# Recurrent heads on one weighted buffer, and modulation units inside the MLP streams

## Chip, cores and metric

The kernel is one launch on one core of a Trainium2 chip. Five engines run side by side: TensorE multiplies matrices from SBUF into PSUM (eight banks), VectorE and ScalarE work on elements, GpSimd does a few element operations, and SyncE issues the DMAs. The metric is the device time of one execution in microseconds (us), lower is better.

## What is computed

Two transformer blocks on 256 tokens of width 2048, all in fp32. The first block has an input projection, a mixing stage (Fourier mixing on half of the width, dilated attention with eight heads on the other), an output projection and an MLP of width 8192. The second has context and latent tokens, a modulation computed from `c`, bidirectional recurrent heads (four GLA heads and four mLSTM heads), and a gated MLP with a 3x3 convolution. Cut to what the change touches:

```python
mod = (c_act @ w_mod + b_mod)                 # 2048 x 12288; the same for c_ctx
sh1, sc1, gt1, sh2, sc2, gt2 = jnp.split(mod, 6, axis=-1)
h = rmsnorm(x, g_norm1) * (1 + sc1) + sh1     # projections q, k, v, gates
# GLA, per direction, head and chunk, a decay per position and channel:
rel = jnp.where(tril, bcum[j] - bcum[i], -inf)
scores[j, i] = sum_k q[j, k] * k[i, k] * exp(rel[j, i, k])
o = scores @ v + (q * exp(bcum)) @ s
s = exp(b_end) * s + (k * exp(b_end - bcum)).T @ v
# mLSTM: the same with one scalar gate per position, a running maximum
# and a normaliser:
s = (q @ k.T) * exp(d_log - m_q)
h = (s @ v + inter * (q @ c)) / max(|den|, exp(-m_q))
y = rmsnorm(o) * g * silu(gate)               # mLSTM: sigmoid(gate)
x = x + gt1 * (y @ w_out)
x = x + gt2 * conv_ffn(rmsnorm(x) * (1 + sc2) + sh2)
```

The modulation does not depend on the first block, so `w_mod` may be read and multiplied at any time before the second block needs it.

## The kernel before

**Streams.** All large products are streams of weight tiles of 128 x 1024 fp32 (512 KB). SyncE asks for each tile in program order into a ring `raw` of eight slots. ScalarE copies it to `whi` (a rounded high part, line 967), VectorE subtracts to `wlo` (line 1289), and TensorE makes three products for each pair (lines 461 to 463: high by high, low by high, high by low). A tile's slot is free again when TensorE has used the tile (`tile_used`), and the ring is one sequence over all streams and fills: the tile at place q waits until the tile at q - 8 is used. A block is 8 tiles. The first MLP consists of four up streams (`up1_0` to `up1_3`) and four down streams (`dn1_0` to `dn1_3`) of 32 tiles each, in blocks of 8.

**Modulation units.** The product with `w_mod` is cut into 48 units. A unit is four unsplit tiles (2 MB): TensorE multiplies them with 16 matmuls of 256 columns into one PSUM bank (`mod_tiles`, line 475), ScalarE copies the row to `modrow` (`mod_rows`, line 975), TensorE turns it into columns (`mod_columns`, line 483), and VectorE adds the bias into `modT` (`mod_adds`, line 1217). Units stand in fills, between streams: 2 at the start, 10 in the mixing stage, 7 ahead of the first MLP, 7 in the context states and 22 in the heads.

**Order.** There is no scheduler: each engine has its program, written by hand, and the engines meet by semaphores. What stands ahead on an engine is done first, also when what stands behind is ready.

**Heads.** `heads2` exists once for each engine. For the GLA heads it goes through 14 levels, seven (`LEVELS`) for each direction z: at level n, blocks of 2L = 2^(n+1) positions are weighted by the decay measured from their middle. VectorE subtracts the middle from the running decay `bT` (line 1512), ScalarE takes the exponential of the negative absolute value (line 1131), VectorE multiplies the queries (`qE`, line 1537) and GpSimd the keys (`kE`, or in `zl`, line 1692), TensorE makes the scores of all four heads and both token tiles (line 801, eight matmuls of 128 x 128), and VectorE takes the masked part of them into `ST` (line 1499). After each level stands one unit. After the seventh level the state that comes from the context is made (lines 827 to 830) and the running decay of the other direction is built (line 779). Then come the GLA output (lines 843 to 845), the q and k transposes and gate rows of the mLSTM heads (lines 708 to 862) and eight mLSTM steps, one for each head and direction. A step broadcasts a head's rows (874), multiplies keys and queries (878), weights them on VectorE (1598, 1605), makes the output (893, 894), scales it on VectorE (1578 to 1588), and has one unit (475) up to the seventh. Then come the gain and gate products (1627) and the transposes for `out2` (582).

## Time and profile before

| | us |
|---|---|
| median of three runs | 2799.53 (2797.16 to 2802.60) |
| the profiled execution | 2801.47 |
| its span on the core | 2799.7 |
| in1, from the first weight product | 29.95 to 213.8 |
| mixing stage | 215.6 to 312.8 |
| ahead of the first MLP | 402.9 to 446.4 |
| first MLP | 446.4 to 1190 |
| heads | 1676.6 to 1927.4 |
| in these, mLSTM steps | 1814.1 to 1903.1 |
| mean granted TensorE clock | 0.965 of full speed |

All numbers are of one profiled execution, apart from the median. In the rows below a timeline row gives the start, the length, the engine, the line of the kernel, the operation with what it writes and reads, and in brackets how long the engine was idle before it and whom it waited for. Several instructions of one kind in succession are one row, with their number behind x. A window row gives the busy time of each engine in a stretch and TensorE's mean granted clock, 1.00 for full speed.

### The profile page before, as it was taken

The numbers are of one execution on the slowest core, as the hardware profiler recorded it, in microseconds if no ns is written. First come the engines' busy times: TensorE is split into PE (matmuls) and PEld (weight loads), VectorE is DVE, ScalarE is ACT, GpSimd is POOL, SyncE is SP. The second block draws the span as 40 slices with busy tenths as digits, with TensorE's granted clock in tenths as the row PEclk, the third lists the DMA queues.
The fourth block names the chain that finished last, engine by engine and source line by source line (L and its number), as shares of the span: only waits on it lengthen the run. The fifth ranks groups of instructions, "written<-read, shape, count | busy, mean of one in ns | idle before, by whom it ended". The sixth has DMA issues, their size and how long they took to land.

```text
span 2799.7 us, 39040 instructions
## 1 busy us (share of the span) xinstructions
PE 2628.4 (94%) x16120; PEld 2254.8 (81%) x16120; DVE 1483.8 (53%) x1836; ACT 1081.7 (39%) x1294; POOL 40.9 (1%) x18
## 2 busy tenths in 40 slices
PE   6999898999999999999799996787989999999997
PEld 4886577989889899778578884556889979998996
DVE  4433435544545545553354436436577766775675
ACT  4433324433434344453344333303433343334333
POOL 0000000000000000000000003200000000000000
PEclk9999998999999999999899998887999999999999
DMA  7552766555555556455545555544535555555554
GB/s 285 192 193 111 295 238 228 183 189 185 187 185 185 188 183 234 151 188 188 214 139 191 192 195 213 190 181 145 186 129 184 183 187 197 183 185 185 184 177 132
DMA packets 143883, 529.17 MB, mean 189 GB/s; under 512 B 16112, under 2 KB 16112, under 8 KB 142464
## 3 DMA queue, kind: packets, MB, share of 16 engines
q1 hardware_dynamic: 143744, 527.17, 54.2%
q8 instruction: 105, 1.72, 0.2%
q14 instruction: 34, 0.28, 0.0%
HBM read 525.01 MB, written 2.10 MB: 188 GB/s over the span
## 4 chain that ended last, share of the span: by engine, by line
PE 88%; DVE 5%; DMA 3%; ACT 2%; issue 1%; SPq 0%; DVEq 0%; ACTq 0%
PE PSA L461 26%; PE PSA L462 26%; PE PSA L463 26%; DMA raw<-in_w_mod 3%; PE PSA L475 2%; PE PSA L801 1%; DVE cv L1267 1%; PE PSA L893 1%; DVE wlo L1289 1%; DVE tpv L1374 1%; PE PSA L582 1%; DMA raw<-in_w_in 1%; ACT whi L967 1%; PE PSA L619 1%; PE PSA L631 0%
## 5 line engine op out<-in xcount | busy, mean ns | idle before, releaser
L1289 DVE TENSOR_TENSOR wlo<-raw,whi 128x1024 fp32r<-128x1024 f32 x788 | 925.5, 1219 | 529.1 <-ACT whi L967 526.4
L967 ACT ACTIVATE whi<-raw 128x1024 fp32r<-128x1024 f32 x788 | 795.2, 1051 | 550.8 <-DMA raw<-in_w_down 209.1
L461 PE MATMUL PSA<-uhi,whi 128*128 128x256 f32 x2400 | 681.8, 284 | 3.2 <-issue 2.8
L462 PE MATMUL PSA<-ulo,whi 128*128 128x256 f32 x2400 | 681.3, 284 | 0.0
L463 PE MATMUL PSA<-uhi,wlo 128*128 128x256 f32 x2400 | 681.3, 284 | 0.0
L461 PEld LDWEIGHTS PSA<-uhi,whi 128*128 128x128 f32 x2400 | 463.0, 193 | 4.6 <-issue 3.4
L462 PEld LDWEIGHTS PSA<-ulo,whi 128*128 128x128 f32 x2400 | 463.0, 193 | 0.2
L463 PEld LDWEIGHTS PSA<-uhi,wlo 128*128 128x128 f32 x2400 | 463.0, 193 | 0.0
L461 PE MATMUL PSA<-whi,uhi 128*128 128x512 f32 x1088 | 432.9, 398 | 27.4 <-DVE wlo L1289 15.5
L462 PE MATMUL PSA<-wlo,uhi 128*128 128x512 f32 x1088 | 430.2, 395 | 0.0
L463 PE MATMUL PSA<-whi,ulo 128*128 128x512 f32 x1088 | 429.7, 395 | 0.0
L461 PE MATMUL PSA<-whi,ahi 128*128 128x512 f32 x856 | 338.4, 395 | 3.6 <-DVE wlo L1289 3.6
L463 PE MATMUL PSA<-whi,alo 128*128 128x512 f32 x856 | 337.8, 395 | 0.0
L462 PE MATMUL PSA<-wlo,ahi 128*128 128x512 f32 x856 | 337.8, 395 | 0.0
L461 PEld LDWEIGHTS PSA<-whi,uhi 128*128 128x128 f32 x1088 | 208.3, 191 | 74.0 <-issue 24.1
L463 PEld LDWEIGHTS PSA<-whi,ulo 128*128 128x128 f32 x1088 | 208.3, 191 | 44.2
L462 PEld LDWEIGHTS PSA<-wlo,uhi 128*128 128x128 f32 x1088 | 208.6, 192 | 43.2
L461 PEld LDWEIGHTS PSA<-whi,ahi 128*128 128x128 f32 x856 | 161.2, 188 | 42.9 <-issue 5.2
L463 PEld LDWEIGHTS PSA<-whi,alo 128*128 128x128 f32 x856 | 161.1, 188 | 37.9
L462 PEld LDWEIGHTS PSA<-wlo,ahi 128*128 128x128 f32 x856 | 161.2, 188 | 37.2
L475 PE MATMUL PSA<-raw,cst 128*32 128x256 f32 x1536 | 113.6, 424 | 46.5 <-DMA raw<-in_w_mod 31.2
L1267 DVE SCALAR_TENSOR_TENSOR cv<-PSA,vec,cv 128x189 f32<-128x189 f32 (+2 forms) x344 | 133.0, 427 | 16.9 <-DVE cv L1258 1.8
(254 smaller groups left out, 1418.8 us busy)
## 6 DMA issues: line engine op xcount, KB each, us to landing
raw<-in_w_up SPq DMA_DIRECT2D x300, 512.0 KB, 3.3
raw<-in_w_in SPq DMA_DIRECT2D x208, 512.0 KB, 3.2
raw<-in_w_mod SPq DMA_DIRECT2D x192, 512.0 KB, 7.1
raw<-in_w_down SPq DMA_DIRECT2D x192, 512.0 KB, 3.2
raw<-in_w_out SPq DMA_DIRECT2D x64, 512.0 KB, 3.2
raw<-in_w_down2b SPq DMA_DIRECT2D x20, 512.0 KB, 3.7
h<-in_x SPq DMA_DIRECT2D x2, 1024.0 KB, 6.2
xc<-in_ctx SPq DMA_DIRECT2D x2, 1024.0 KB, 9.1
```

Source lines behind the costliest of these rows:

```text
L461: pe.matmul(dst, xh, wh, start=start, stop=False)
L462: pe.matmul(dst, xh, wl, start=False, stop=False)
L463: return pe.matmul(dst, xl, wh, start=False, stop=stop)
L475: mm = pe.matmul(PSA[32 * j:32 * j + 32, bank, 0:UW], cst[:, 2 * k:2 * k + 32], raw[:, q % SLOTS, j * UW:(j + 1) * UW], start=t == 0, stop ...
L582: mm = pe.transpose(PSA[:, banks[n % 4], kk * TOK + t * P:kk * TOK + (t + 1) * P], src, ident)
L619: mm = pe.matmul(PSA[:, c, :], z1[:, t, s * 256 + c * P:s * 256 + (c + 1) * P], cB("dft_pos")[:, t * 512:(t + 1) * 512], start=t == 0, sto ...
L801: mm = pe.matmul(PSA[:, b0 + c // 4, (c % 4) * P:(c % 4 + 1) * P], lk(hd, slice(t * P, (t + 1) * P)), lq[:, hd, t * P:(t + 1) * P], start= ...
L893: pe.matmul(dst[:, c], WW[:, r % 2, t, jc * P:(jc + 1) * P], rhs, start=n == 0, stop=False)
L967: AF(whi[:, n % SLOTS, 0:w], raw[:, n % SLOTS, 0:w], ACT.Copy).then_inc(hi_done, 1)
L1267: last = STT(cvv[n][:, ro, co], gate[n][:, ri, ci], cwv[:, ck + n, tap:tap + 1], cvv[n][:, ro, co], ALU.mult, ALU.add)
L1289: TT(wlo[:, n % SLOTS, 0:w], raw[:, n % SLOTS, 0:w], whi[:, n % SLOTS, 0:w], ALU.subtract).then_inc(lo_done, 1)
L1374: ins = TS(buf[:, n % 2, kk * TOK:(kk + 1) * TOK], PSA[:, banks[n % 4], kk * TOK:(kk + 1) * TOK], A[:, k:k + 1], (Bc[:, k:k + 1] if Bc is ...
```

## The change

**Units.** 28 of the 48 units go into the streams of the first MLP, one in each block of `up1_0` to `up1_3` and `dn1_0` to `dn1_2`. SyncE asks for the unit's four tiles behind main tile 3 of the block, TensorE multiplies them behind main tile 3, and makes the columns behind tile 5; ScalarE copies the row and VectorE adds behind their split of tile 7, and TensorE waits for the add ahead of the next block's first unit tile. The fills at the start, in the mixing stage and ahead of the first MLP are gone. The states have 6 units, the heads 14: thirteen in the GLA levels, one in the mLSTM steps.

**Heads.** The running decays of both directions are built at the start. In a level one half of each block has its query weighted, the other its key, by the same exponential with its own sign; both halves go to one buffer `XX`, which is both operands of the scores. VectorE writes them in two half operations, GpSimd has no program any more, the copy into `ST` takes a half. The states from the context, the mLSTM gate rows and the q and k transposes stand between the levels. The mLSTM steps also hold the gate times gain products, the squares, the gated outputs, the transposes for `out2` and the first six of its weight splits. The product with the gate columns (`gate_rows`) moves into `out2`, behind its tile 6. Some buffers move to the area of `whi`.

The pieces below are, in turn: the plan, SyncE in a stream, TensorE in a stream behind a tile's products, TensorE's levels, VectorE's weighting in a level, VectorE in the mLSTM steps, and GpSimd.

```diff
+UNIT = 4
 GLA_UNITS = 13
-Y_UNIT = 20
-UNIT = 4
+MLSTM_UNITS = 1
...
-    ph = [Fill("fill_start", (4, 6)), Phase("in1", "tok", 4, 2, 8, k=KD, evac="z1"), Fill("fill_mix", (0, 1, 2, 3) * 2 + (0, 1)),
-          Phase("out1", "tok", 2, 2, 8, k=KD, evac="res"), Fill("fill_mlp", (4, 6) * 3 + (4,))]
+    ph = [Phase("in1", "tok", 4, 2, 8, k=KD, evac="z1"), Phase("out1", "tok", 2, 2, 8, k=KD, evac="res")]
     for q in range(GROUPS1):
-        ph.append(Phase(f"up1_{q}", "feat", 2, 2, 8, evac="up1"))
-        ph.append(Phase(f"dn1_{q}", "tok", 2, 2, 8, k=16, evac="res"))
+        ph.append(Phase(f"up1_{q}", "feat", 2, 2, 8, evac="up1", units_from=0))
+        ph.append(Phase(f"dn1_{q}", "tok", 2, 2, 8, k=16, evac="res", units_from=0 if q < GROUPS1 - 1 else None))
     ph.append(Phase("inC", "tok", 3, 2, 8, k=KD, evac="zc", dest=6))
-    ph.append(Fill("fill_states", (4, 5, 4, 5, 4, 6, 4)))
+    ph.append(Fill("states", 6))
     ph.append(Phase("inL", "tok", 6, 2, 8, k=KD, evac="zl"))
-    ph.append(Fill("fill_heads", (4, 5) * 6 + (4,) + (6, 7) * 3 + (6,) + (4, 6)))
+    ph.append(Fill("heads", GLA_UNITS + MLSTM_UNITS))
...
+                            if p.has_unit(i) and t == UNIT - 1:
+                                for j in range(UNIT):
+                                    tile(t_in["w_mod"][UNIT * p.unit_no(i, b) + j], p, i, p.unit_at(b, j))
...
+                            if p.has_unit(i):
+                                if t == 0:
+                                    if not isinstance(i, int) or p.unit_no(i, b):
+                                        pe.wait_ge(mini_done, p.unit_no(i, b))
+                                if t == UNIT - 1:
+                                    for j in range(UNIT):
+                                        q = p.unit_at(b, j)
+                                        mod_tile(4, q % SLOTS, p.plus_tiles(16 * (q // SLOTS + 1), i, 2), j)
+                                if t == UNIT + 1:
+                                    mod_columns(4, p.unit_no(i, b))
...
+            for m in range(2 * LEVELS):
+                pe.wait_ge(B["qe_done"], m + 1)
+                if m >= 2:
+                    pe.wait_ge(B["lv_done"], m - 1)
+                scores(XX[:, m % 2, :, :], XX[:, m % 2, :, :], 2 if m % 2 else 6).then_inc(B["lv_ready"], 1)
+                if m >= 2:
+                    mod_columns(5, heads.unit0 + m - 2, apart=True)
...
+                if m >= 1:
+                    fill_tiles(heads, m - 1, 4)
...
+                    for second in range(2):
+                        src = gqT if second != z else gkT
+                        ins = TT(half_blocks(XX[:, m % 2, :, :], L, m % 2)[second], half_blocks(src[:, :, :], L, m % 2)[second],
+                                 half_blocks(EEs[m % 2], L, m % 2)[second], ALU.mult)
...
+                    if s == 2:
+                        scales(0)
+                        gate_times_gain(4)
+                    if 2 <= s <= MLSTM_UNITS + 1:
+                        mod_adds(7, heads.unit0 + GLA_UNITS + s - 2)
...
-                pool.wait_ge(B["e_exp"], m + 1)
-                dst = kE[:, :, :] if m % 2 == 0 else zl[:, :, 0, :].rearrange("p a (b t) -> p a b t", b=2)
-                by_two = "p (a b) t -> p a b t"
```

TensorE at the beginning of the heads; lines 801 before and 845 after are scores, 475 and 512 a unit's tiles, 483 and 522 its columns. Before:

```order
L779 MATMUL PSA<-ca,LA 128x128 x8
L789 MATMUL PSA<-ca,zl 128x128 x16
L801 MATMUL PSA<-gqT,gkT 128x128 x8
L801 MATMUL PSA<-qE,kE 128x128 x8
L475 MATMUL PSA<-raw,cst 32x256 x16
L801 MATMUL PSA<-qE,zl 128x128 x8
L475 MATMUL PSA<-raw,cst 32x256 x16
L483 MATMUL PSA<-ca,modrow 128x2 x2
```

and now:

```order
L830 MATMUL PSA<-ca,LA 128x128 x8
L837 MATMUL PSA<-ca,zl 128x128 x16
L830 MATMUL PSA<-ca,LA 128x128 x8
L845 MATMUL PSA<-gqT,gkT 128x128 x8
L845 MATMUL PSA<-XX 128x128 x8
L850 MATMUL PSA<-LA,ca 128x512 x2
L845 MATMUL PSA<-XX 128x128 x8
L512 MATMUL PSA<-raw,cst 32x256 x16
L746 MATMUL PSA<-ca,gm 8x128
```

The second direction's running decay (the second 830) and the key decays (850) have moved to the opening, the gate rows (746) between the levels, and the columns now stand behind the next scores.

VectorE in one of the GLA levels. Before:

```order
L1512 TENSOR_TENSOR EE<-bT 128x1024
L1537 TENSOR_TENSOR qE<-gqT,EE_118 128x1024
L1499 COPY_PREDICATED ST<-levels,PSA 128x1024
L1217 TENSOR_TENSOR modT<-PSA,vec 128x4
L1512 TENSOR_TENSOR EE_118<-bT 128x1024
```

and now, with work of the mLSTM's prelude (1648, 1649, 1670 to 1672) between:

```order
L1617 TENSOR_TENSOR zl<-bT 128x2x512
L1627 TENSOR_TENSOR XX<-gkT,EE 128x32x16
L1627 TENSOR_TENSOR XX<-gqT,EE 128x32x16
L1643 COPY_PREDICATED ST<-levels,PSA 128x64x8
L1325 TENSOR_TENSOR modT<-PSA,vec 128x4
L1670 TENSOR_SCALAR rows_125<-rows_125 8x256
L1671 TENSOR_TENSOR rows_125<-rows_125 8x256
L1672 COPY rows_125<-rows_125 8x256
L1617 TENSOR_TENSOR EE<-bT 128x1024
```

Each of the two multiplies and the copy covers half of the elements, in pieces.

ScalarE ahead of the first MLP. Before:

```order
L941 ACTIVATE junk_85,part<-h 128x512 x2
L1020 ACT_TABLE_LOAD
L1020 ACTIVATE stat<-stat 128x2
L975 ACTIVATE modrow<-PSA 128x256 x7
L967 ACTIVATE whi<-raw 128x1024 x2
L1033 ACTIVATE uhi<-tpv 128x512 x8
```

and now:

```order
L1008 ACTIVATE junk_85,part<-h 128x512 x2
L1089 ACT_TABLE_LOAD
L1089 ACTIVATE stat<-stat 128x2
L1034 ACTIVATE whi<-raw 128x1024 x2
L1102 ACTIVATE uhi<-tpv 128x512 x8
L1034 ACTIVATE whi<-raw 128x1024 x6
L1041 ACTIVATE modrow<-PSA 128x256
```

The seven row copies no longer stand ahead of the first weight copies; one stands behind the eighth copy of the block.

## Rows read from the trace of the kernel before

**Rows 1.** The page's fourth part: the chain that ended last, by engine.

```profile
PE 88%; DVE 5%; DMA 3%; ACT 2%; issue 1%; SPq 0%; DVEq 0%; ACTq 0%
```

**Rows 2.** Windows: us, PE, PEld, DVE, ACT, POOL busy, PEclk, DMA share, GB/s.

```profile
402.90:446.40 43.50, 31.57 (x285) 14.44 (x285) 14.20 (x29) 10.56 (x20) 0.00 (x0) 0.75 0.89 351
446.40:1190.00 743.60, 741.81 (x4682) 671.25 (x4683) 382.58 (x346) 313.43 (x323) 0.00 (x0) 1.00 0.55 185
1676.60:1927.40 250.80, 186.95 (x1445) 138.30 (x1443) 124.46 (x214) 72.79 (x120) 40.67 (x14) 0.84 0.51 190
1814.10:1903.10 89.00, 76.40 (x460) 52.57 (x460) 30.76 (x95) 7.05 (x15) 0.00 (x0) 0.79 0.49 180
```

**Rows 3.** Timeline of TensorE, GLA levels: start, length in us, operation, wait.

```profile
1689.12 3.78 PE L801 MATMUL PSA<-qE,kE 128*128 128x128 f32 x16 [4.92 <-DVE qE L1537]
...
1701.63 2.02 PE L801 MATMUL PSA<-qE,kE 128*128 128x128 f32 x16 [1.75 <-issue]
1703.59 1.93 PE L475 MATMUL PSA<-raw,cst 128*32 128x256 f32 x32
1705.45 0.61 PE L483 MATMUL PSA<-ca,modrow 128*128 128x2 f32 x4
...
1712.21 2.02 PE L801 MATMUL PSA<-qE,kE 128*128 128x128 f32 x16 [1.60 <-issue]
...
1743.52 3.75 PE L801 MATMUL PSA<-qE,zl 128*128 128x128 f32 x16 [8.13 <-issue]
```

**Rows 4.** Timeline of TensorE, end of the mixing stage.

```profile
306.69 0.64 PE L475 MATMUL PSA<-raw,cst 128*32 128x256 f32 x8 [0.63 <-DMA raw<-in_w_mod]
...
312.87 0.76 PE L461 MATMUL PSA<-whi,uhi 128*128 128x512 f32 x1 [2.43 <-DVE wlo L1289]
```

**Rows 5.** Timeline of VectorE, the program's start.

```profile
14.57 2.48 DVE L1383 TENSOR_SCALAR xn<-h,stat 128x2048 f32<-128x2048 f32 x2
22.95 4.77 DVE L1289 TENSOR_TENSOR wlo<-raw,whi 128x1024 fp32r<-128x1024 f32 x4 [5.90 <-ACT whi L967]
```

**Rows 6.** Timeline of VectorE, attention heads of the mixing stage.

```profile
261.72 0.68 DVE L1426 SCALAR_TENSOR_TENSOR lg<-PSA,bias 128x512 f32<-128x512 f32 x1
...
267.95 0.69 DVE L1426 SCALAR_TENSOR_TENSOR lg<-PSA,bias 128x512 f32<-128x512 f32 x1 [2.45 <-PE PSA L659]
...
271.32 0.42 DVE L1438 TENSOR_TENSOR ulo<-PSA,uhi 128x256 fp32r<-128x256 f32 x1
```

**Rows 7.** Timeline of VectorE, ahead of the first MLP stream.

```profile
407.47 2.48 DVE L1383 TENSOR_SCALAR xn<-h,stat 128x2048 f32<-128x2048 f32 x2
...
437.03 2.36 DVE L1289 TENSOR_TENSOR wlo<-raw,whi 128x1024 fp32r<-128x1024 f32 x2
```

**Rows 8.** Timeline of VectorE, after the context states.

```profile
1388.24 2.36 DVE L1289 TENSOR_TENSOR wlo<-raw,whi 128x1024 fp32r<-128x1024 f32 x2 [5.19 <-ACT whi L967]
```

**Rows 9.** VectorE's groups by line and shape: busy us, mean ns.

```profile
L1537 DVE TENSOR_TENSOR qE<-gqT,EE 128x1024 f32<-128x1024 f32 x14 | 22.0, 1569 | 13.5 <-ACT EE L1131 6.9 <-PE PSA L801 6.6
...
L1484 DVE TENSOR_TENSOR WK<-zc,wcol 128x512 f32<-128x512 f32 x4 | 2.5, 688 | 0.0
```

**Rows 10.** Timeline of TensorE, the GLA output.

```profile
1789.31 0.70 PE L843 MATMUL PSA<-zl,ST 128*128 128x256 f32 x2 [0.26 <-DVE modT L1217]
...
1801.46 1.91 PE L852 MATMUL PSA<-ca,zl 128*128 128x128 f32 x16
```

**Rows 11.** Timeline of TensorE, one mLSTM step and the pauses around the steps.

```profile
1812.68 1.02 PE L862 MATMUL PSA<-ca,rows 8*128 8x8 f32 x8 [7.47 <-DVE rows L1567]
...
1869.99 1.93 PE L475 MATMUL PSA<-raw,cst 128*32 128x256 f32 x32 [2.32 <-DVE modT L1217]
...
1874.41 1.03 PE L893 MATMUL PSA<-zl,WW 128*128 128x256 f32 x4
...
1879.99 1.93 PE L475 MATMUL PSA<-raw,cst 128*32 128x256 f32 x32 [2.25 <-DVE modT L1217]
...
1923.10 3.58 PE L582 MATMUL PSA<-ca,zl 128*128 128x128 f32 x16 [9.50 <-DVE zl L1627]
```

More of the change, by code:

```diff
@@ L78, in __init__ @@
         self.per_iter = self.per_block * blocks
-class Fill:
-    def __init__(self, name, banks):
-        self.name, self.banks, self.units = name, banks, len(banks)
-    def before(self, u):
-        same = [v for v in range(u) if self.banks[v] == self.banks[u]]
-        return self.unit0 + (same[-1] + 1 if same else 0)
+        self.units_from = iters if units_from is None else units_from
+        self.units = (iters - self.units_from) * blocks
+        self.unit_tiles = UNIT * blocks if self.units else 0
@@ L731, in _, with states_unit @@
             mm.then_inc(B["suf_ready"], 1)
-            mod_units(BY["fill_states"], range(3), fresh=True)
+            states = BY["states"]
+            def states_unit(u, before=None):
+                fill_tiles(states, u, STATE_BANKS[u])
+                if before is not None:
+                    mod_columns(STATE_BANKS[before], states.unit0 + before)
+            pe.wait_ge(mini_done, states.unit0)
+            states_unit(0)
+            states_unit(1, 0)
+            pe.wait_ge(mini_done, states.unit0 + 1)
+            states_unit(2, 1)
             pe.wait_ge(B["mr_rev"], 1)
@@ new lines, in first_state @@
+            def first_state(z):
+                pe.wait_ge(B["kt_done"], z + 1)
+                for hd in range(H):
+                    mm = pe.matmul(PSA[:, hd // 2, (hd % 2) * DV:(hd % 2 + 1) * DV], (kte1 if z else kte)[:, hd * DK:(hd + 1) * DK],
+                                   zl[:, z, 8 + hd // 2, (hd % 2) * DV:(hd % 2 + 1) * DV], start=True, stop=True)
+                mm.then_inc(B["s1_ready"], 1)
+            heads = BY["heads"]
+            pe.wait_ge(B["gm_done"], 2)
+            running_decay(0, 6)
@@ L836, in _, with broadcast_rows @@
+            def broadcast_rows(s):
+                src = rows2[:, 9:11, ::-1] if s >= 4 else rows2[:, 9:11, :]
+                pe.matmul(PSA[:, s % 2, :], ident[0:8, s:s + 1].broadcast_to([8, P]), src, start=True, stop=True).then_inc(B["bc_ready"], 1)
+            pe.wait_ge(B["s1_done"], 2)
+            broadcast_rows(0)
             pe.wait_ge(B["lv_done"], 2 * LEVELS)
@@ L989, in gates, with stream @@
                     AF(TM[:, :], TM[:, :], ACT.Ln, bias=1.0).then_inc(B["abs_done"], 1)
-            def stream(p, first, between={}):
+            def stream(p, first, between={}, early=0):
                 def body(i):
@@ L996, in body @@
                                 first[-1]()
-                            split(p, i, b * p.per_block + t)
+                            if not (isinstance(i, int) and i == 0 and b == 0 and t < early):
+                                split(p, i, b, t)
                             if isinstance(i, int) and i == 0 and b == 0 and t in first:
@@ L1316, in gates_end, with stream @@
                 ins.then_inc(B["gm_done"], 1)
-            def stream(p, first, between={}):
+            def stream(p, first, between={}, early=0):
                 def body(i):
@@ L1323, in body @@
                                 first[-1]()
-                            split(p, i, b * p.per_block + t)
+                            if not (isinstance(i, int) and i == 0 and b == 0 and t < early):
+                                split(p, i, b, t)
                             if isinstance(i, int) and i == 0 and b == 0 and t in first:
@@ L1358, in transposes_lo @@
                 buf = tpy if j in (2, 4) else tpv
[L1359 removed]
+                banks = tp_banks(j)
                 def low(n):
@@ new lines, in heads2 @@
+                dve.wait_ge(B["dg_done"], 1)
+                for m in range(1, 2 * LEVELS):
+                    if m + 1 < 2 * LEVELS:
+                        from_mid(m + 1)
+                    weigh(m)
+                    take(m - 1)
+                    if m >= 3:
+                        mod_adds(5, heads.unit0 + m - 3)
+                    if m in between:
+                        between[m]()
+                take(2 * LEVELS - 1)
+                mod_adds(5, heads.unit0 + GLA_UNITS - 2)
```

775 lines of the change are left out of this document (423 added, 352 removed).

## Prediction, made before the changed kernel had run

> **What bounds the kernel now.** I read the chain of waits first: 88% of it is TensorE and 3% is DMA [rows 1], so time comes back only where TensorE stands still, and every matmul that is put where it never stands still costs its own length. The stretches say which is where [rows 2]. In the first MLP stream TensorE is busy 741.8 of 743.6 us: no gap. In the stretch between its inputs and that stream (402.9 to 446.4) it is busy 31.6 of 43.5 us at a mean clock of 0.75, with DMA at 0.89: the work there is modulation units, and they run at the pace of their tiles. In the heads (250.8 us) it is busy 187 us at a clock of 0.84, DMA 0.51, and inside them the mLSTM steps have 0.79. The clock has two levels, 1.2 and 2.4 GHz, and a mean below 1 says that part of the work is done at the lower one after a pause.
>
> **What one modulation unit costs, by place.** Between scores a unit takes TensorE 1.86 us for its 16 products and 0.61 for its columns, 2.5 together [rows 3]. Back to back it is bound by DMA: a w_mod tile takes TensorE 0.64 and makes it wait 0.63 [rows 4], so 1.28 a tile and 5.1 a unit. So 4.4 is gained wherever a unit leaves a place in which only units run (less what is prefetched), and 2.5 is paid wherever it enters a full TensorE stream.
>
> **The change part by part.** Gains:
>
> Start, 5.7. Two units go. VectorE ends its normalization at 17.05 and then waits 5.90 for ScalarE's copies, which stand behind the units; its four weight splits end at 27.7 [rows 5]. Without the units they can follow at once: 17.05 + 4.77 = 21.8, so 5.9, of which I take 5.7 since the first copy has still to be made. Bounds 3 and 6.
>
> Mix, 30. Ten units go. A head of attention takes VectorE 3.8 us (267.95 to 271.74), the one in hand begins at 261.72 [rows 6]. Three more heads and that one: 261.7 + 4 x 3.8 = 276.9; transposes, last products and the wait for the first split (the 2.4 of rows 4 among them) 5.3, so out1 begins at 282.2. It began at 312.87, after tiles that waited for DMA: 30.7, taken as 30. Bounds 24 and 31.
>
> MLP prelude, 27. Seven units go. VectorE's normalization ends at 409.95 and its splits begin at 437.03 [rows 7], with nothing but unit adds between; 27.1. Copies and transposes are there before. Bounds 20 and 27.
>
> States, 5. One unit fewer (seven to six) and a better place for the last: the split waits 5.19 [rows 8]. Bounds 0 and 5.
>
> Heads, 91. I build the time after from pieces. Opening: the first weighted scores began at 1689.12, 12.5 after the stage began [rows 3]; the second direction's sums (as many products as a group of scores, 2 us) come ahead, 15. Levels: before, two took 10.58 (1701.63 to 1712.21), 5.3 each. Now TensorE has scores 1.96, unit 1.86 and columns 0.61, 4.4; VectorE has a full subtraction 1.2 (a split's time, 4.77 / 4, rows 5), two halves and a half copy at 0.69 (a 128x512 operation's time, rows 9), 3.3, plus the add, 3.5. So TensorE bounds them: 13 x 4.4 = 57. Extra pieces between levels (states, gate rows, two transposes of q and k, columns, 10 groups, together some 5 lengths of a scores group): 10.5. That is 68 us for thirteen units, and DMA needs 66 less the two prefetched: it just suffices. GLA's output 12, as it was from 1789.31 on [rows 10]. mLSTM's prelude 5: most of it now lies between levels, where TensorE before waited 7.47 for gate rows [rows 11]. Eight mLSTM steps: one took 10.0 (1869.99 to 1879.99); its unit took 2.4 and about 0.8 of the 2.25 in which TensorE waited for the add behind VectorE's output goes too, 6.8. It can't go much below 5.5: products of the output take TensorE 3.3 (1874.41 to 1877.74) and the output with its add VectorE 2.25, in sequence where they share banks. 8 x 6.8 = 54. Tail 2: the stretch after the last step (with its wait of 9.50 for the gated outputs, rows 11, and two units) goes, since squares, gains and the first splits stand in the steps and out2's first four tiles cover the rest. Sum 15 + 57 + 10.5 + 12 + 5 + 54 + 2 = 156, against 250.8: 95, less 4 for the gate rows that move into out2's stream. Bounds: 70 (levels at 5.3, steps at 7.6, tail 6) and 105.
>
> What vanishes in the levels is thus little (5.3 to 4.4). The gain is the switch of direction (TensorE waited 8.13 in it, rows 3), the mLSTM prelude, and the units in the steps.
>
> All gains: 5.7 + 30 + 27 + 5 + 91 = 159.
>
> Cost: 28 units in MLP streams that have no gap, 28 x 2.5 = 70. ScalarE's row copy and VectorE's add are not on the path: VectorE is busy 383 and ScalarE 313 of 743.6 us there [rows 2], the add stands two or three tiles ahead of the matmul that needs its bank. SP's queue is passed too: four w_mod tiles go ahead of main tiles 4 to 7 of a block, so a block asks for 12 tiles; at 1.28 each that is 15.4 of the 25.7 us that it lasts (743.6 / 32 blocks and the unit). Ring slots are eight, and the unit's four are free again once TensorE has passed them, so main tiles still arrive a few microseconds early. Bounds: 2.4 and 5.1 (a unit fully at the pace of its tiles); zero or below is excluded because TensorE has 1.8 us free in 743.6. I take 2.5, since the tiles can be asked for a block's half ahead.
>
> Net 89. The profiled execution took 2801.5, with 1.8 around its span; it lies 1.9 above the median of the runs. 2801.5 − 89 = 2712.5; by the median 2710.6, so **2711**.
>
> **Where the skill bears on it.** VectorE's halves are read and written in runs of 1 to 64 elements, and no row here has such a form. The Trainium skill (SBUF — State Buffer, section Door 1: The DMA port swizzle, its note on cachelines) says that fp32 in SBUF may be strided by up to four elements for free, but that PSUM's lines are two values, so non-contiguous reads there slow down. By that only the shortest levels' copies out of PSUM grow, by about 0.6 x 4, 2 to 3 us in all; the general case is rival E. On GpSimd: VectorE's multiply of 128x1024, made in the levels in which GpSimd works, had a mean of 1.57 us [rows 9], a split of that size 1.19 [rows 5]; the same page's section Who interferes with whom states that a VectorE operation with two SBUF inputs contends with a GpSimd one that reads SBUF. The trace agrees, and the change leaves GpSimd without work; the lengths of 1.2 and 0.69 above already suppose that.
>
> **Rivals.**
>
> B, the clock. The units that are taken out also kept TensorE awake. With them the mLSTM steps had 0.79 and the heads 0.84 [rows 2]. Without them TensorE pauses for VectorE in every step. If it stays at the low level, a step's 2.0 of rows and scores (10.0 less 2.4, 3.3 and 2.25) and its 3.3 of output products become 10.6, in place of 6.8: +30, and mix +5; time 2746. For it: the low clock stands just where pauses stand. Against: a pause in a step is about 1.5 us. The Trainium skill (TensorE: Matmul & The Clock Gate, section HAM oscillation — how this bites in real kernels) describes matmul groups that start slow after each wait; by it the case would be as just priced. Chance 0.15.
>
> E, broken shapes. If a half costs VectorE as much as a whole, a level has 4 x 1.2 + 0.15 = 5.0, with the handshakes that the old pitch also held over its operations, 5.7, and 13 x 1.3 = 17 more: 2728. Chance 0.11.
>
> C, dear units in the streams. If w_mod tiles come late or the add delays the next unit, a unit costs 4 us: +42, 2753. For it: a busy wait of TensorE on one queue for raw tiles while its split tiles are ready. Chance 0.12.
>
> D, slower than before. The ring serves tiles in one order, and a slot is free only when TensorE has used it; a unit's tile asks in turn for the slot of the main tile ahead. If the stream comes to stand on that once a block, a unit costs its four tiles at the pace of DMA, 5.1, and the time of one main tile, 743.6 / 256 = 2.9, together 8, and the sum turns: 28 x 8 = 224 against 159, 2866. It decides from 159 / 28 = 5.7 us a unit. Against: eight slots are 23 us of main work. Chance 0.04.
>
> F, the heads do not get shorter by more than half of what I say (one engine's order makes each piece between levels a stop for all): 91 becomes 45, 2757. Chance 0.06.
>
> The forecast has 0.52.
>
> **How the numbers follow.** Low end: my bounds upward, 10 in the heads, 3 in mix and start, 3 of the units, some lower still: 2690. High end: B, E and C lie in up to 2756; 2758 leaves out D and part of F, and below 2690 about 0.05. A measurement of this kernel can tell some 0.2% or 5.6 us; no case lies within that of 2799.5, so same 0.01, slower 0.04 for D plus 0.01 for what I don't see, faster 0.94.
>
> **What would show it.** In the profile of the changed kernel: the first MLP stream longer by 28 x 2.5 = 70 (spread over four groups), with waits at products for splits below 1 us a block; if DMA stands as what releases the unit's products there, C or D. Out1 begins 36 us earlier than before; MLP prelude some 16 us long. The heads 156 us: levels 4.4 apart (5.7 is E), mLSTM steps 6.8 (over 9 with a clock near 0.5 is B). If the gap between heads and out2 is over 6 us my tail is wrong. I'm wrong on the whole if the streams grow by over 110 or the heads shrink by under 60.

## The result, and the profile after

| | before | after |
|---|---|---|
| median of four runs, us | 2800.19 (2797.16 to 2802.60) | 2702.16 (2699.78 to 2704.64) |
| span of the profiled execution | 2799.7 | 2698.5 |

The ratio is 0.9651, 95% interval 0.9634 to 0.9667: 98 us less, where 89 were forecast. The page of the changed kernel, busy time and the chain that ended last (answering to [rows 1]):

```profile
span 2698.5 us, 39013 instructions
...
PE 2588.6 (96%) x16120; PEld 2239.1 (83%) x16120; DVE 1472.2 (55%) x1852; ACT 1076.1 (40%) x1297; POOL 0.2 (0%) x4
...
PE 89%; DVE 6%; ACT 2%; DMA 1%; issue 1%; DVEq 0%; SPq 0%; ACTq 0%
```

GpSimd has no work left, and DMA has gone from 3% of the chain to 1%. Where the time went shows best where TensorE's timeline enters each stage. The first product of in1, out1, the first MLP, inC (the context projection), inL (the latent one), out2 and the second MLP:

```profile
24.32 0.80 PE L503 MATMUL PSA<-whi,uhi 128*128 128x512 f32 x1 [2.97 <-DVE ulo L1474]
...
277.48 0.76 PE L503 MATMUL PSA<-whi,uhi 128*128 128x512 f32 x1 [2.77 <-DVE wlo L1397]
...
383.68 0.35 PE L503 MATMUL PSA<-uhi,whi 128*128 128x256 f32 x1 [1.57 <-issue]
...
1189.09 0.39 PE L503 MATMUL PSA<-whi,uhi 128*128 128x512 f32 x1
...
1395.73 0.77 PE L503 MATMUL PSA<-whi,uhi 128*128 128x512 f32 x1 [0.61 <-issue]
...
1826.16 0.80 PE L503 MATMUL PSA<-whi,uhi 128*128 128x512 f32 x1 [2.18 <-DVE zl L1728]
...
1942.30 0.55 PE L503 MATMUL PSA<-uhi,whi 128*128 128x256 f32 x1 [1.69 <-issue]
```

The same products stood at 29.95, 312.87, 446.41, 1180.56, 1393.11, 1927.45 and 2043.33 before, which gives this table (us, a negative number is time saved):

| stretch | before | after | change | forecast |
|---|---|---|---|---|
| start to in1 | 29.95 | 24.32 | -5.6 | -5.7 |
| in1 and mixing | 282.92 | 253.16 | -29.8 | -30 |
| out1 and what follows it | 133.54 | 106.20 | -27.3 | -27 |
| first MLP | 734.15 | 805.41 | +71.3 | +70 |
| inC and states | 212.55 | 206.64 | -5.9 | -5 |
| inL and heads | 534.34 | 430.43 | -103.9 | -95 |
| out2 to the second MLP | 115.88 | 116.14 | +0.3 | +4 |
| second MLP to the end | 756.37 | 756.20 | -0.2 | 0 |

They add up to -101.2, the difference of the spans. Windows of the changed kernel's first MLP, its whole heads, its levels and its mLSTM steps (us, busy time of PE, PEld, DVE, ACT, POOL, then TensorE's mean clock, DMA share, GB/s), which answer to [rows 2]:

```profile
383.70:1189.00 805.30, 801.16 (x5648) 700.97 (x5649) 389.75 (x373) 327.66 (x347) 0.00 (x0) 1.00 0.66 242
1674.30:1826.10 151.80, 140.83 (x1145) 109.84 (x1143) 103.49 (x213) 58.90 (x111) 0.00 (x0) 0.97 0.54 210
1686.80:1756.60 69.80, 67.45 (x750) 50.51 (x750) 54.40 (x90) 27.95 (x49) 0.00 (x0) 1.00 0.90 354
1772.00:1822.50 50.50, 45.55 (x241) 35.52 (x239) 38.32 (x103) 14.69 (x33) 0.00 (x0) 0.91 0.12 42
```

The first MLP runs from its own first product to inC's; the table of before ended it at 1190, which takes in 9.4 us of inC. TensorE is as full there as it was, 801 of 805 us, now with 28 units in it; it waits three times (1.57, 2.38 and 1.74 us), never for DMA. The heads' window begins 4.5 us ahead of their first product at 1678.77; from there to out2 TensorE is busy 136 of 147 us at a mean clock of 0.96, where it was busy 187 of 251 at 0.84. In the mLSTM steps the clock went from 0.79 to 0.91. The levels are at full clock, with DMA at 0.90.

How far can one profile be trusted? The same program was profiled again as a control (below), and most kernels of the experiments leave most stages as they are. In1 and mixing took 251.7 to 253.8 us in the nine profiles without idle matmuls there. The first MLP took 804.2 us in the control and in three more with all 28 units, and 805.4 in two (the wait of 2.38 above is 0.88 in the control). InC and the states with six units and no idle matmuls took 204.3 to 209.2. So differences of a microsecond mean something in the first MLP, and little in the states.

### The profile page after: what moved, and what is told of

Same layout as the page of the kernel before. It is cut to its first block, busy times and chain, and to the rows that moved or that the text cites. A ratio compares the mean times of both kernels' runs of the same rounds, so it can differ in the third digit from the quotient of the medians.

```text
span 2698.5 us, 39013 instructions
## 1 busy us (share of the span) xinstructions
PE 2588.6 (96%) x16120; PEld 2239.1 (83%) x16120; DVE 1472.2 (55%) x1852; ACT 1076.1 (40%) x1297; POOL 0.2 (0%) x4
## 4 chain that ended last, share of the span: by engine, by line
PE 89%; DVE 6%; ACT 2%; DMA 1%; issue 1%; DVEq 0%; SPq 0%; ACTq 0%
PE PSA L503 27%; PE PSA L504 26%; PE PSA L505 26%; PE PSA L512 3%; DMA raw<-in_w_mod 1%; DVE wlo L1397 1%; DVE cv L1375 1%; DVE tpv L1485 1%; PE PSA L845 1%; PE PSA L522 1%; PE PSA L664 1%; PE PSA L633 1%; PE PSA L676 1%; ACT whi L1034 1%; PE PSA L958 0%
## 5 line engine op out<-in xcount | busy, mean ns | idle before, releaser
L505 PEld LDWEIGHTS PSA<-whi,ulo 128*128 128x128 f32 x1088 | 207.3, 191 | 43.9
L1020 ACT ACTIVATE sl<-cv 128x512 f32<-128x512 f32 (+1 forms) x22 | 13.7, 623 | 259.3 <-DVE cv L1375 259.3
```

The lines of the kernel that those rows point to most:

```text
L505: return pe.matmul(dst, xl, wh, start=False, stop=stop)
```

## The experiments

**What a unit costs in a full stream.** A block of a down stream (`dn1`) lasts 24.8 us in the changed kernel and was 22.3; one of an up stream (`up1`) lasts 25.5 and was 23.0. Both are 2.5 longer. A unit's matmuls in `up1_1`, and its columns:

```profile
651.82 1.93 PE L512 MATMUL PSA<-raw,cst 128*32 128x256 f32 x32
...
659.54 0.50 PE L522 MATMUL PSA<-ca,modrow 128*128 128x2 f32 x4
```

Is that TensorE's own time, or the tiles and the place in the ring (rivals C and D)? First I left out 9 of the 16 matmuls of each of the 28 units, and kept everything else:

```diff
-                for j in range(4):
+                for j in range(3 if trim and t else 0, 4):
```

> The changed kernel (2702.2 us) with 9 of the 16 matmuls of each of the 28 units in the MLP streams left out (their part of the modulation is not computed); tiles, row copies, columns and adds stay. Theory, a unit in a stream costs TensorE's own time: a matmul of a unit takes 1.86 / 16 = 0.116 us, 28 x 9 x 0.116 = 29 us less, 2673 us, each block 1.05 us shorter. Rival, a unit's price is its tiles or the place in the ring: no change, 2702 us.

Measured 2702.94 us, ratio 0.9639 (0.9623 to 0.9656), no change. By the text on record that was the rival's answer. The row says otherwise:

```profile
649.38 1.93 PE L512 MATMUL PSA<-raw,cst 128*32 128x256 f32 x14
```

It is the same 1.93 us, with 14 records in place of 32 (each of these matmuls leaves two records, so 7 in place of 16). The four matmuls of a tile, each on its own 32 columns of the array, run side by side, so the three that were left out of a tile shorten nothing. (The Trainium skill, TensorEngine Tiling (Array Packing), section Key Properties, states that different tiles of the array can execute in parallel; the trace agrees, 1.93 us for 7 as for 16.) The experiment hadn't touched the chain that it meant to. So I shortened the chain of the four tiles: in the second to fourth, each matmul goes over 32 columns and not 256 (that part of the modulation is left out).

```diff
-                    mm = pe.matmul(PSA[32 * j:32 * j + 32, bank, 0:UW], cst[:, 2 * k:2 * k + 32], raw[:, slot, j * UW:(j + 1) * UW],
+                    mm = pe.matmul(PSA[32 * j:32 * j + 32, bank, 0:w], cst[:, 2 * k:2 * k + 32], raw[:, slot, j * UW:j * UW + w],
...
-                                        mod_tile(4, q % SLOTS, p.plus_tiles(16 * (q // SLOTS + 1), i, 2), j)
+                                        mod_tile(4, q % SLOTS, p.plus_tiles(16 * (q // SLOTS + 1), i, 2), j, 32 if j else UW)
```

> The changed kernel with the matmuls of the second, third and fourth tile of each of the 28 units in the MLP streams cut from 256 to 32 columns (their part of the modulation is not computed); tiles, row copies, columns and adds stay. Leaving out 9 of 16 matmuls had changed nothing, as the four column groups of a tile seem to run side by side; this cut shortens the chain of four itself. Theory, TensorE's own time: a tile takes 0.46 us, three of four shrink to 0.1 or less, 28 x 1.1 = 31 us less, ratio to before about 0.953. Rival, the price is the tiles' or the place in the ring: no change, ratio 0.964.

Measured 2672.55 us, ratio 0.954 (0.9525 to 0.9554).

```profile
664.06 0.83 PE L512 MATMUL PSA<-raw,cst 128*32 128x256 f32 x32
```

The unit went from 1.93 to 0.83, and the first MLP takes 774.8 us, where the control takes 804.2: 29.5 less. 28 x 1.10 is 30.8, and two new waits for ScalarE's row copy (0.88 and 0.25) take most of the rest. All tiles were still fetched. So the price of a unit in a stream is the length of its chain on TensorE; rivals C and D are out.

**Units put back into a place of their own.** The edit takes 8 units from `dn1_1` and `dn1_2` and makes them between out1 and the first MLP, in the way of the kernel before:

```diff
+    ph.append(Fill("mlp", 8))
-        ph.append(Phase(f"dn1_{q}", "tok", 2, 2, 8, k=16, evac="res", units_from=0 if q < GROUPS1 - 1 else None))
+        ph.append(Phase(f"dn1_{q}", "tok", 2, 2, 8, k=16, evac="res", units_from=0 if q < GROUPS1 - 3 else None))
```

> The changed kernel with 8 of the 28 units taken from the streams (dn1_1 and dn1_2) and put between out1 and the first MLP, where 7 stood before. Theory, full TensorE streams charge 2.54 a unit and a place in which only units run charges DMA's pace behind the two that are prefetched: 6 x 5.3 = 32 more ahead of the MLP, 8 x 2.54 = 20 less in the streams, +12, 2714 us. Rival, a unit's price in a stream is hidden to a good part by something else (the streams give back under half): +22 or more, 2724 us or more.

Measured 2715.47 us, ratio 0.9689 (0.9672 to 0.9705). From out1's first product to the MLP's it took 137.5 us, and 105.2 in the control: 32.3 more. The MLP took 784.3 and 804.2: 20.0 less. Both terms are as worked out (32 and 20).

**The mLSTM prelude as one piece again.** Gate rows, transposes, gate columns and their chains go back behind the GLA output:

```diff
-                if m == 1:
-                    gate_matrix_rows(1, 0)
-                if m == 3:
-                    transposed(1, 0, B["mt_ready"])
-                if m == 5:
-                    transposed(7, 0, B["mt_ready"])
...
             mod_columns(5, heads.unit0 + GLA_UNITS - 1, apart=True)
+            gate_matrix_rows(1, 0)
+            transposed(1, 0, B["mt_ready"])
+            transposed(7, 0, B["mt_ready"])
```

> The changed kernel with the mLSTM prelude (gate rows, q and k transposes, gate columns and their chains on VectorE and ScalarE) put back behind the GLA output, as one piece, as it stood before the change; all else stays. Theory, it now fills the order of the levels and its pauses were the cost: the prelude's stretch is again some 13 us, the levels lose 5 us of TensorE work, +7, 2709 us. Rival 1, the levels are bound by w_mod tiles (DMA 0.94 there), so nothing comes back there: +13, 2715 us. Rival 2, the pauses are not what the change gained: within 2 us of 2702.

Measured 2713.74 us, ratio 0.9678 (0.9661 to 0.9694). Two rows of TensorE's timeline in it, with their waits (those of the other two pieces are 0.77 and 0.32):

```profile
1766.27 1.09 PE L837 MATMUL PSA<-ca,zl 128*128 128x128 f32 x8 [1.11 <-ACT mqT L1234]
1768.86 0.66 PE L921 MATMUL PSA<-ca,rows 8*128 8x8 f32 x8 [1.51 <-DVE rows L1670]
```

From the GLA output's first product to the first output of an mLSTM step it took 26.0 us, and 15.4 in the changed kernel: +10.6. The levels, from the first weighted scores to the GLA output, took 67.7 in place of 69.8: only 2.2 of some 5 us of TensorE work came back there. So +8.4 is the prelude, between the theory (+7) and rival 1 (+13): that fits levels held by tiles in part (the DMA share is 0.90 there). Levels and prelude took 69.3 to 70.4 and 15.0 to 15.8 us in all profiles of the changed order, so these two differences stand clear. Something else was in this profile too, which none of the three had:

```profile
1776.50:1803.00 26.50, 25.86 (x145) 19.24 (x144) 19.41 (x56) 6.28 (x15) 0.00 (x0) 0.95 0.22 80
1803.00:1836.30 33.30, 30.43 (x99) 23.73 (x97) 18.15 (x45) 7.49 (x17) 0.00 (x0) 0.55 0.00 1
```

These windows are the mLSTM steps of this run: halfway TensorE's clock fell from 0.95 to a mean of 0.55. Measured from the first output's first product to the end of the last output, the steps took 61.3 us, where they took 52.0 in the changed kernel's profile. Their order had not been changed. The changed kernel run once more (the control, below), measured in the same way:

```profile
1769.46:1826.25 56.79, 51.86 (x249) 40.43 (x247) 39.30 (x104) 15.79 (x37) 0.00 (x0) 0.83 0.11 38
```

So one program's steps took 52.0 us at a clock of 0.91 and 56.8 at 0.83. The median of this run stands 11.6 us above the changed kernel's. The 8.4 of the prelude are the part of it that was made on purpose; how much of the rest is the prelude's place and how much is chance in the steps, one profile can't tell.

**The late part of the gates ahead of out2.** All gated outputs and transposes come before out2's first product, and out2's first splits behind them (VectorE's and ScalarE's programs are changed to match):

```diff
-            stream(BY["out2"], u0=32, between={(0, 1): lambda: transposes(4, (4, 5)), (0, 2): lambda: transposes(4, (6, 7)),
-                                               (0, 6): gate_rows_2})
+            transposes(4, (4, 5))
+            transposes(4, (6, 7))
+            stream(BY["out2"], u0=32, between={(0, 6): gate_rows_2})
```

> The changed kernel with the second half of the gated outputs, all their transposes and the first splits of out2 ahead of out2's first product, as before the change, instead of beside its first tiles and steps. Theory, the tail was a wait of TensorE for VectorE (9.5 us before): out2 begins 10 to 14 us later, +10, 2712 us. Rival, the steps' VectorE work that is saved in exchange gives most of it back: +3, 2705 us.

Measured 2709.97 us, ratio 0.9672 (0.9656 to 0.9688).

```profile
1824.89 3.65 PE L633 MATMUL PSA<-ca,zl 128*128 128x128 f32 x16 [6.63 <-issue]
1833.18 0.76 PE L503 MATMUL PSA<-whi,uhi 128*128 128x512 f32 x1 [4.64 <-DVE wlo L1391]
```

The two waits, 6.63 and 4.64, are back between the last step and out2. InL and heads together took 441.8 us against 430.4, +11.4, and out2 gave back 2.0, as two groups of transposes left it. The trace says +9.4, close to the theory's +10. The steps took 52.0 us, as they did with the splits in them, so the rival's exchange isn't there. By the medians it is 7.8 us; the intervals of the two ratios overlap, so the time alone is no proof.

**Better places for units, and the clock.** Four kernels on one chip, the changed one among them.

> The changed kernel itself, run beside the next three so that they are compared on one chip: 2702 us, and its mLSTM steps again at a mean clock of 0.91 to 1.0. If the steps can fall to the lower level here as they did in the run with the prelude apart, this run is some 9 us longer in them.

Measured 2702.60 us, ratio 0.9641 (0.9628 to 0.9654).

The second takes 4 units from `dn1_2`; two go between the last attention heads, two behind out1:

```diff
+    ph = [Phase("in1", "tok", 4, 2, 8, k=KD, evac="z1"), Fill("mix", 2), Phase("out1", "tok", 2, 2, 8, k=KD, evac="res")]
+    ph.append(Fill("mlp", 2))
...
+                if s >= 9:
+                    mod_columns(2 * (s - 9), BY["mix"].unit0 + s - 9)
+                if s in (7, 8):
+                    fill_tiles(BY["mix"], s - 7, 2 * (s - 7))
```

> The changed kernel with 4 units taken from the streams (dn1_2): two go between the last attention heads of the mixing stage, two between out1 and the first MLP, where TensorE waits 7 us; in both places the ring holds just these two units ahead. Theory, a unit costs nothing where it is prefetched and TensorE waits: 4 x 2.54 = 10 less in the streams, 0 to 3 more in the pauses, -8 against the control. Rival, the ring then holds no weight tile of the next stream, which starts later: +0 to +5.

Measured 2692.01 us, ratio 0.9605 (0.9592 to 0.9618): 10.6 less than the control, and the intervals don't meet.

```profile
367.46 3.23 PE L513 MATMUL PSA<-raw,cst 128*32 128x256 f32 x56
...
373.28 0.61 PE L523 MATMUL PSA<-ca,modrow 128*128 128x2 f32 x4 [0.53 <-ACT modrow L1055]
374.59 2.79 PE L634 MATMUL PSA<-ca,xn 128*128 128x128 f32 x16 [0.70 <-DVE xn L1513]
```

The two units behind out1 lie where TensorE waited 7.06 us for the norm in the changed kernel; 0.70 of that wait is left. From out1's first product to the MLP's it took 106.6 us (control 105.2), and the MLP took 794.0 (804.2): 1.5 lost, 10.2 gained. Out1 began at 277.44 (277.71), so the two in the mixing stage cost nothing that can be seen.

The third puts matmuls of no use into TensorE's waits:

```diff
+            def warm(n, bank):
+                for _ in range(n):
+                    pe.matmul(PSA[:, bank, 0:P], ident, ident, start=True, stop=True)
```

> The changed kernel with idle matmuls (128x128, results unread) in TensorE's waits: 11 at the start, 10 ahead of out1, 48 ahead of the first MLP, 40 ahead of inL, 32 ahead of up2, and 33 in the last mLSTM steps. Theory, the lower clock after these waits lies on the path: the 12 first products of in1 and of out1 take 0.40 and not 0.63 (2.5 us each), transposes and first products of the others 1 to 2 each, the late steps never fall: -8 against the control, clock 0.99. Rival, VectorE's chain ends each of these waits and its next steps hide the slow products: within 2 us of the control.

Measured 2700.51 us, ratio 0.9639 (0.9626 to 0.9652), 2 us below the control and within its interval.

```profile
272.11 2.39 PE L532 MATMUL PSA<-ca 128*128 128x128 f32 x20
275.04 0.47 PE L503 MATMUL PSA<-whi,uhi 128*128 128x512 f32 x1 [0.54 <-DVE wlo L1410]
...
1924.94 7.41 PE L532 MATMUL PSA<-ca 128*128 128x128 f32 x64 [0.78 <-DVE gtb L1827]
```

and two windows, its mLSTM steps and the 32 idle matmuls ahead of the second MLP:

```profile
1767.13:1818.67 51.54, 51.38 (x315) 42.25 (x313) 38.51 (x103) 14.72 (x33) 0.00 (x0) 0.97 0.11 41
1924.90:1932.30 7.40, 7.36 (x66) 7.36 (x67) 3.15 (x6) 0.20 (x1) 0.00 (x0) 1.00 0.01 2
```

Ahead of out1 it gained: out1 begins with a product of 0.47 and at full clock after it, and from in1's first product to out1's it took 251.3 us. The four kernels with these idle matmuls took 251.0 to 251.3, and the nine without 251.7 to 253.8, so this gain of about 2 us is real.

Ahead of the second MLP there were too many. The 32 took 7.41 us at a granted clock of 1.00, 0.23 each, and the wait that they had to fill was 4.44: from out2 to the second MLP 119.2 us, 2.6 more than in the control. In the mLSTM steps they held the clock at 0.97. What that is worth shows only beside all profiles of this order of steps (us from the first output to the end of the last):

| idle matmuls in the steps | steps | clock |
|---|---|---|
| none, seven profiles (one without the first splits in the steps) | 51.9, 52.0, 52.0, 54.0, 54.3, 56.4, 56.8 | 0.91, 0.91, 0.91, 0.87, 0.87, 0.83, 0.83 |
| none, the prelude behind the levels | 61.3 | 0.74 |
| 33, four profiles | 51.1, 51.5, 51.6, 53.4 | 0.98, 0.97, 0.97, 0.94 |

The idle matmuls raise the clock in every profile, but the steps get hardly shorter than where they go well by themselves: against the control it is 5.3 us, against the changed kernel's first profile 0.5. Over the whole program the mean clock of this kernel's five executions was 0.987 to 0.989 and the control's 0.980 to 0.983, for 2 us.

The fourth has five units in the mLSTM steps:

```diff
-MLSTM_UNITS = 1
+MLSTM_UNITS = 5
-        ph.append(Phase(f"dn1_{q}", "tok", 2, 2, 8, k=16, evac="res", units_from=0 if q < GROUPS1 - 1 else None))
+        ph.append(Phase(f"dn1_{q}", "tok", 2, 2, 8, k=16, evac="res", units_from=0 if q < GROUPS1 - 2 else None))
```

> The changed kernel with five units in the mLSTM steps in place of one, and four fewer in the streams. Theory, a unit costs its own length in a step as in a stream and the last add delays the first transposes by 2: 10 less in the streams, 12 more in the steps, +2 against the control. Rival, units keep the clock up in the steps (rival B of the prediction): the steps' clock is 1.0, -3 or less.

Measured 2700.19 us, ratio 0.9635 (0.9622 to 0.9648), the control's within both intervals.

```profile
1757.30:1822.50 65.20, 60.43 (x386) 45.71 (x384) 39.40 (x108) 15.81 (x37) 0.00 (x0) 0.82 0.44 162
```

By the measure of the table the steps took 66.6 us, 9.8 more than the control's, and the streams 10.2 less. With five units the clock was 0.82, not 1.0: units don't keep it up there. The medians, 2.4 us apart, say that a unit costs here about what it costs in a stream; the steps alone differ by 5 us between profiles and can't say it closer.

**Together.** Units in pauses, and idle matmuls only at the start (11), ahead of out1 (10) and in the last steps (33):

> The four units in pauses (-10 measured) together with idle matmuls only where the run with all of them gained: 11 at the start, 10 ahead of out1, 33 in the last mLSTM steps. Theory, the gains add up: 2 at the start, 2 at out1, 0 to 6 in the steps (as far as they would have fallen to the lower clock), so 2692 - 6 = 2686 us, ratio 0.958 to 0.959. Rival, units in the pauses have warmed these places already: 2691 us, ratio 0.960.

Measured 2687.84 us, ratio 0.9589 (0.9576 to 0.9603). The profiled span is 2682.9. That is in the theory's range, but the interval overlaps that of the four units alone (0.9592 to 0.9618), so the time doesn't decide between theory and rival. In the profiles the 2 us ahead of out1 are there; the steps' gain is 0 to 5 us, as the table says.

Then two more units in the states, two fewer in `dn1_1`:

```diff
-    ph.append(Fill("states", 6))
+    ph.append(Fill("states", 8))
```

> The kernel of the run before with two more units in the context states, whose TensorE waits 4.3 us for gate rows and 6.1 us for the norm, and two fewer in the streams (dn1_1). Theory, 2 x 2.54 = 5 less in the streams and 0 to 2 more in the states: -4 against the run before. Rival, the states are at DMA's pace (waits for w_mod tiles of 0.6 and 1.7 us there), so each extra unit costs 5.1: +5.

Measured 2687.03 us, ratio 0.9585 (0.9571 to 0.9598): not to be told from the one before. The first MLP gave 5.0 back, and from inC's first product to inL's it took 211.2 in place of 207.3, 3.9 more; that stage differs by up to 5 us between profiles of one order, so the rows have to say why. TensorE, then ScalarE and VectorE:

```profile
1373.41 0.61 PE L523 MATMUL PSA<-ca,modrow 128*128 128x2 f32 x4 [0.53 <-ACT modrow L1069]
1379.28 0.77 PE L504 MATMUL PSA<-whi,uhi 128*128 128x512 f32 x1 [5.26 <-DVE ulo L1509]
...
1372.97 0.38 ACT L1069 ACTIVATE modrow<-PSA 128x256 f32<-128x256 f32 x1 [6.50 <-PE PSA L523]
1373.26 1.99 ACT L1062 ACTIVATE whi<-raw 128x1024 fp32r<-128x1024 f32 x2
...
1374.40 1.22 DVE L1432 TENSOR_TENSOR wlo<-raw,whi 128x1024 fp32r<-128x1024 f32 x1 [5.40 <-ACT whi L1062]
```

A new wait of 5.26 us ahead of inL (0.61 in the kernel before). ScalarE's second row copy waited for the first unit's columns, which stood behind the transposes, and ScalarE's first weight copies stood behind it. The last kernel makes the columns ahead of the transposes:

```diff
-            transposes(3, range(4))
-            mod_columns(4, states.unit0 + 6)
+            mod_columns(4, states.unit0 + 6)
+            mod_columns(6, states.unit0 + 7)
+            transposes(3, range(4))
```

> The kernel with eight units in the states, with the columns of the last two units made ahead of the transposes for inL and not behind them, so that ScalarE's second row copy no longer holds its copies of inL's first weight tiles (TensorE waited 5.3 us there). Theory, the two added units cost the states 3.9 because of that order: inL begins 3 us earlier, ratio to before 0.957 to 0.9575. Rival, the wait was DMA's (the ring refilled behind the two units): no change, ratio 0.9585.

```profile
1375.33 0.76 PE L504 MATMUL PSA<-whi,uhi 128*128 128x512 f32 x1 [1.26 <-issue]
```

The wait is 1.26. From the start of VectorE's normalization to inL's first product it takes 7.47 us, as with six units, where it took 12.84 with the columns behind the transposes. So the order on ScalarE's queue cost 5.4 us, and DMA had no part in it. InC to inL takes 206.5 us, within what six units take: the two added units cost the states nothing that these profiles can tell. The median is 2682.20 us (2679.61 to 2687.67), the ratio 0.9583 (0.9569 to 0.9597), which by itself can't tell it from the two before. All three are faster than the changed kernel (0.9641 and 0.9651); this one by 0.6%.

## Why the prediction was right, and where it was not

**The account by place held.** Start, mixing stage, what stands ahead of the MLP, streams and states came out within 1.3 us each (5.6, 29.8, 27.3, 71.3 and 5.9 against 5.7, 30, 27, 70 and 5). That is closer than profiles of one program agree in the mixing stage and the states, so the last microsecond is luck; by the control the streams took 70.1. The two prices, 2.5 for a unit in a full stream and 5.1 to 5.4 where only units run behind the prefetched ones, were shown apart by the run with eight units put back, and the first one's cause by the narrow units. The bounds of 2.4 and 5.1 had left the ring open as a cause; it isn't one.

**The heads were mis-sized by 8.** Built from 15 + 67.5 + 12 + 5 + 54 + 2 = 156, they took 147.4:

```profile
1678.77 1.95 PE L830 MATMUL PSA<-ca,LA 128*128 128x128 f32 x16
...
1682.31 1.95 PE L830 MATMUL PSA<-ca,LA 128*128 128x128 f32 x16
1684.32 2.02 PE L845 MATMUL PSA<-gqT,gkT 128*128 128x128 f32 x16
1686.77 2.05 PE L845 MATMUL PSA<-XX 128*128 128x128 f32 x16 [0.42 <-DVE XX L1627]
```

The term that was mis-sized is the opening. I took the old 12.5 and added the new sums' 2. It is 8.0 (1678.77 to 1686.77). The old one held waits of 1.85 and 4.92 (for VectorE's copy and product, the latter in [rows 3]), and 0.42 of wait is left. The sums of the other direction (the second row of line 830) stand in them, which accounts for 2 of the 6.5 us; a piece that moves into a stretch with waits takes their place, it isn't added. The other 4.5 are on VectorE, whose order I had not priced. Before, and now:

```profile
1684.23 1.23 DVE L1522 SCALAR_TENSOR_TENSOR ST<-PSA,ca 128x1024 f32<-128x1024 f32 x1 [2.21 <-PE PSA L801]
1685.49 2.43 DVE L1512 TENSOR_TENSOR EE<-bT 128x1024 f32<-128x1024 f32 x1
1687.85 1.21 DVE L1537 TENSOR_TENSOR qE<-gqT,EE 128x1024 f32<-128x1024 f32 x1
```

```profile
1685.40 0.71 DVE L1627 TENSOR_TENSOR XX<-gkT,EE 128x512 f32<-128x512 f32 x1
1686.01 0.70 DVE L1627 TENSOR_TENSOR XX<-gqT,EE 128x512 f32<-128x512 f32 x1
1686.61 1.23 DVE L1696 SCALAR_TENSOR_TENSOR ST<-PSA,ca 128x1024 f32<-128x1024 f32 x1
```

Before, VectorE waited for the unweighted scores and took them into `ST` ahead of the first weighting; now it weights first. This is read from the rows; no run took the two parts of the opening apart. Levels with what stands between them took 69.8 against 67.5, and what held them isn't taken apart either; GLA output and prelude 15.4 against 17; the steps, to their end at 1824.0, 52 against 54; the tail 2.2 against 2.

**The gate rows in out2** were put at 4 and cost 0.3. They take their 4 (the first row below), but in the trace of before (the second) out2 waited 3.74 us at 1944.23 for a split, and 0.34 of that wait is left now (the third).

```profile
1849.16 3.73 PE L646 MATMUL PSA<-ca,modT 128*128 128x128 f32 x32
...
1944.23 0.77 PE L461 MATMUL PSA<-whi,uhi 128*128 128x512 f32 x1 [3.74 <-DVE wlo L1289]
...
1843.62 0.47 PE L503 MATMUL PSA<-whi,uhi 128*128 128x512 f32 x1 [0.34 <-DVE wlo L1397]
```

I had not looked at that wait. The heads' 8.4 and these 3.7 are the 12 us by which the net was too small (101.2 against 89 in the profiles; 98 against 89 by the medians).

**Rival B, the clock,** is a real mechanism, but the change didn't bring it and its price is smaller. I took it that the removed units kept TensorE awake. The steps' clock was 0.79 with seven units, 0.83 to 0.91 in seven profiles with one, and 0.82 with five, so units don't keep it up. The waits beside them (2.25 and 2.32 per step in [rows 11]) may be what lets it fall; no run shows that. What it costs varies from run to run: 51.9 to 61.3 us for steps of one order, so 0 to 9 us and not 30. (The price of 30 also left out the pause of 1.5 us that a step of 6.8 holds, so by its own terms it was too low.) What decides in which step the clock falls, these runs don't show.

**Rivals C, D and F** are out: a unit costs 2.54, by its own chain, and the heads shrank by more than forecast.

**Rival E, broken shapes,** is out except in one place. One of VectorE's groups by line (busy us, mean ns), and three copies out of PSUM on its timeline:

```profile
L1627 DVE TENSOR_TENSOR XX<-gkT,zl 128x512 f32<-128x512 f32 x7 | 4.8, 685 | 0.0
```

```profile
1690.23 1.30 DVE L1643 COPY_PREDICATED ST<-levels,PSA 128x512 f32<-128x512 uint8 x1
1693.68 1.31 DVE L1643 COPY_PREDICATED ST<-levels,PSA 128x512 f32<-128x512 uint8 x1
1700.09 0.70 DVE L1643 COPY_PREDICATED ST<-levels,PSA 128x512 f32<-128x512 uint8 x1
```

A half multiplies in 0.685 us at every level, down to runs of one element. The copy of a half out of PSUM takes 1.30 at blocks of one and two elements and 0.70 from four on; these are levels 1 and 2 of either direction, 4 x 0.6. The Trainium skill's page SBUF — State Buffer (section Door 1: The DMA port swizzle) says that PSUM's lines hold two fp32 values and that any non-contiguous pattern there slows down matmuls; it doesn't speak of VectorE. On VectorE the trace agrees for runs of one and two, and shows no cost for runs of four, which are not contiguous either. The mask is read in the same broken form, and no run keeps the two apart.

**GpSimd's absence** shows too. The multiply of [rows 9] took 1.57 on average in a whole, two halves now take 1.37. The 1.57 is a mixture: ten of the 14 took 1.21 to 1.23 and four took 2.41 to 2.45. Each of the four began while a GpSimd multiply that had started 1.0 to 1.3 us earlier was running. One of them, in the trace of before:

```profile
1702.54 2.49 POOL L1692 TENSOR_TENSOR zl<-gkT,EE 128x1024 f32<-128x1024 f32 x1 [1.00 <-ACT EE L1131]
...
1703.69 2.42 DVE L1537 TENSOR_TENSOR qE<-gqT,EE 128x1024 f32<-128x1024 f32 x1 [0.90 <-PE PSA L801]
```

In seven others VectorE began 0.04 us ahead of GpSimd: there VectorE took 1.23, and GpSimd 3.40 in place of 2.4. The later one waits. The subtraction of 2.43 in the old opening is the same case (its GpSimd multiply began at 1684.50).

## What to carry to other kernels

Price a piece of work by the place where it stands: in a full TensorE stream it costs its own chain, in a run of its own kind it costs the pace of its data, and in a wait that it fits it costs nothing. The best places are the last ones, and there are few: two prefetched units in each of two waits brought another 10 us (a third in one wait was not tried). When a piece moves into a stretch, look first for the waits of that stretch and take them off. And before a stage is read from one profile, look at how far profiles of one program differ in it.

## What the runs showed that I had not expected

- The four matmuls of a unit's tile, on 32 columns each, run side by side: 7 of 16 take the same 1.93 us as 16. Cutting their moving columns from 256 to 32 for three tiles of four gives 0.83.
- In one program's mLSTM steps the clock's mean was 0.91 in one execution and 0.83 in another, 52.0 and 56.8 us, and in a kernel with the same steps it fell to 0.55 from the middle on, 61.3 us. Thirty-three idle matmuls in the waits held it at 0.94 to 0.98, and the steps at 51.1 to 53.4.
- Idle matmuls aren't free at full clock either: 32 of them took 7.41 us at a granted clock of 1.00, and where the wait was 4.44 they cost more than the clock gave back.
- Two-input operations of VectorE and GpSimd took turns: a VectorE multiply of 128x1024 that began while GpSimd's was running took 2.4 us and not 1.2.
